# Forgetting-attention layer of a streaming trunk on one core: every matmul on 128 rows and columns, one softmax for four heads' new tokens, z before the next q, and output transpositions beside the last chunks

## The reference

```python
def fox_attend(q, f_q, q_pos, k, v, f_k, k_pos):
    s = jnp.einsum('bqhd,bkhd->bhqk', q, k).astype(jnp.float32) * (B_HEAD_DIM ** -0.5)
    s = s + jnp.transpose(f_q, (0, 2, 1))[..., :, None] - jnp.transpose(f_k, (0, 2, 1))[..., None, :]
    s = jnp.where(k_pos[None, :] <= q_pos[:, None], s, -jnp.inf)
    p = jax.nn.softmax(s, axis=-1)
    return jnp.einsum('bhqk,bkhd->bqhd', p.astype(v.dtype), v)

def fox_layer(x, ...):
    q, z = jnp.split(rmsnorm(x, norm_g) @ w_in, 2, axis=-1)      # w_in 2048 x 4096
    q = rmsnorm(q.reshape(bsz, seq, B_HEADS, B_HEAD_DIM), q_norm_g)  # 16 heads of 128
    ...
    y = (o * jax.nn.silu(z)) @ w_out                              # w_out 2048 x 2048
    return x + y.astype(x.dtype)
```

## Time and profile before

| | |
|---|---|
| median of 3 runs | 1923.48 us (1923.11 to 1923.82) |
| profiled execution: its own time | 1920.44 us |
| its span (first to last instruction) | 1918.6 us |
| PE busy | 1840.1 us (96% of the span) |
| DVE, ACT, POOL busy | 1074.2, 828.8, 290.3 us |
| mean granted TensorE clock (1 is 2.4 GHz) | 0.976 |
| first and last product matmul of the attention layer | 1409.6 and 1907.5 us |

### The profile page before, as it was taken

How to read it: one execution, slowest core, us unless ns; L and a number is a source line. 1 busy time by engine, 2 the same in 40 slices (tenths; PEclk the granted TensorE clock), 3 DMA queues, 4 the chain that set the end, 5 groups by cost and what they waited for, 6 DMA issues and landing times. The chain is left out here.

```text
span 1918.6 us, 29975 instructions
## 1 busy us (share of the span) xinstructions
PE 1840.1 (96%) x12128; PEld 1675.5 (87%) x12128; DVE 1074.2 (56%) x2021; ACT 828.8 (43%) x1406; POOL 290.3 (15%) x569
## 2 busy tenths in 40 slices
PE   4999999999998999999999999999979999999998
PEld 2998889988887999999999899999977798989877
DVE  4565546554546666667757667554355355454544
ACT  4344344534444434434524435545544353443432
POOL 1001111111132321322321210211010000000000
PEclk9999999999999999999999999999989799999998
DMA  3454445644484665655656644465672354535422
GB/s 103 153 169 156 158 142 162 190 144 154 123 249 138 213 211 169 219 190 173 222 175 188 211 132 141 153 212 160 209 248 88 95 157 128 161 107 158 140 75 72
DMA packets 243305, 309.28 MB, mean 161 GB/s; under 512 B 13864, under 2 KB 219456, under 8 KB 242864
## 3 DMA queue, kind: packets, MB, share of 16 engines
q1 hardware_dynamic: 213232, 213.35, 36.4%
q0 software_dynamic: 29232, 91.24, 14.0%
q10 hardware_dynamic: 704, 2.79, 0.5%
HBM read 260.53 MB, written 46.79 MB: 160 GB/s over the span
## 5 line engine op out<-in xcount | busy, mean ns | idle before, releaser
L157 DVE TENSOR_TENSOR w_lo<-raw,w_hi 128x1024 fp32r<-128x1024 f32 x400 | 484.4, 1220 | 421.9 <-ACT w_hi L152 420.4
L152 ACT ACTIVATE w_hi<-raw 128x1024 fp32r<-128x1024 f32 x400 | 412.1, 1053 | 125.4 <-PE acc L177 118.3
L175 PE MATMUL acc<-xg_hi,w_hi 128*128 128x304 f32 x1024 | 315.9, 308 | 4.7 <-DVE w_lo L157 4.7
L177 PE MATMUL acc<-xg_hi,w_lo 128*128 128x304 f32 x1024 | 309.3, 302 | 0.0
L176 PE MATMUL acc<-xg_lo,w_hi 128*128 128x304 f32 x1024 | 309.2, 302 | 0.0
L104 POOL TENSOR_TENSOR cell<-cell 1x1 f32<-1x1 f32 x154 | 65.3, 424 | 1314.8 <-issue 282.5
L175 PEld LDWEIGHTS acc<-xg_hi,w_hi 128*128 128x128 f32 x1024 | 193.3, 189 | 7.9 <-DVE w_lo L157 6.0
L176 PEld LDWEIGHTS acc<-xg_lo,w_hi 128*128 128x128 f32 x1024 | 194.0, 189 | 0.8
L177 PEld LDWEIGHTS acc<-xg_hi,w_lo 128*128 128x128 f32 x1024 | 193.6, 189 | 0.0
L175 PE MATMUL acc<-xb_hi,w_hi 128*128 128x288 f32 x512 | 157.2, 307 | 8.7 <-DVE xb_lo L2340 8.7
L175 PE MATMUL acc<-xk_hi,w_hi 128*128 128x304 f32 x512 | 157.7, 308 | 3.7 <-DVE xk_lo L1879 3.7
(11 more groups left out here) (471 smaller groups left out, 3777.3 us busy)
## 6 DMA issues: line engine op xcount, KB each, us to landing
raw<-in_a_w_in SPq DMA_DIRECT2D x128, 512.0 KB, 4.0
raw<-in_a_w_out SPq DMA_DIRECT2D x64, 512.0 KB, 4.5
raw<-in_w_kvf SPq DMA_DIRECT2D x64, 512.0 KB, 4.5
raw<-in_b_w_in SPq DMA_DIRECT2D x64, 512.0 KB, 3.8
raw<-in_b_w_out SPq DMA_DIRECT2D x32, 512.0 KB, 3.6
raw<-in_a_wq SPq DMA_DIRECT2D x16, 512.0 KB, 4.1
raw<-in_a_wk SPq DMA_DIRECT2D x16, 512.0 KB, 3.6
raw<-in_a_wv SPq DMA_DIRECT2D x16, 512.0 KB, 4.4
```

The lines of the kernel that those rows point to most:

```text
L152: act.activation(w_hi[:, s, :, :], raw[:, s, :, :], ACT.Copy).then_inc(hi_made, 1)
L157: dve.tensor_tensor(w_lo[:, s, :, :], raw[:, s, :, :], w_hi[:, s, :, :].bitcast(F32), ALU.subtract).then_inc(lo_made, 1)
L175: pe.matmul(acc[b][:, 0:width], wh, x_hi[:, k0 + k, :], start=st, stop=False)
L177: mm = pe.matmul(acc[b][:, 0:width], wl, x_hi[:, k0 + k, :], start=False, stop=last and k == 3)
```

## The change

- Order of chunks: q_0, then for each group z_g, OUT_(g-1) (none for g = 0), q_(g+1) (none for g = 3), and OUT_3 at the end. Group g's events now lie in slots 0 to 14 from the first z chunk on.
- The new tokens' scores of four heads are one event Y: q of head x is put into zero-padded columns (`q_new2`), so that its 128-column weights give rows 32x to 32x+31, and the four heads accumulate in one bank. One softmax (EY, NY) and one set of five transpositions (TY) serve all four heads. X takes the place of S and forms the prompt scores alone.
- T has five full 128 x 128 transpositions; O has two matmuls of 256 columns, four of 32 and one of 160.
- The third block of q holds tokens 160 to 287 (128 rows) in place of 32 rows; b uses three banks in place of five; f uses 12 `scalar_tensor_tensor` in place of six `tensor_tensor`.
- All four K events come in slots 1 and 2.
- The last group's high and low parts (H) go to buffers of their own and lie in slots 9 to 15; the others' in slots 0 and 1 of the next group.
- The 48 transpositions of the result are four events y0 to y3 beside the last eight chunks, in the `aux` banks, with no block between.

```diff
-        BESIDE = {8: ["q"], 9: ["r"], 10: ["n"], 11: ["f"], 12: ["K0"], 13: ["b"], ...
+        BESIDE = {0: "q", 1: "r n K0 K1", 2: "f K2 K3", 3: "b", 4: "X0 Y", 5: "E0 EY", 6: "N0 NY X1",
+                  7: "T0 E1 TY", 8: "z O0 N1 X2", 9: "T1 E2", 10: "O1 N2 X3", 11: "T2 E3", 12: "O2 N3", 13: "T3",
+                  14: "O3"}
+        PARTS_NEXT = {0: "H0 H1", 1: "H2 H3"}
+        PARTS_LAST = {9: "H0", 11: "H1", 13: "H2", 15: "H3"}
+        Y_OUT = {2: "y0", 4: "y1", 6: "y2", 7: "y3"}
...
                 def q_finals(g):
...
-                    for t, (_, n) in enumerate(QT):
-                        y = qst[0:n, 3, GRP * t:GRP * (t + 1)].unsqueeze(2).to_broadcast([n, GRP, P])
-                        own.done(dve.tensor_tensor(head_parts(q_t[0:n, t, :], n), head_parts(q_t[0:n, t, :], n), y, ALU.mult))
-                    own.wait()
-                    for t, (_, n) in enumerate(QT):
-                        dve.tensor_tensor(q_t[0:n, t, :], q_t[0:n, t, :], gq[0:n, :], ALU.mult).then_inc(q_final, 1)
+                    for t in range(3):
+                        for m in range(GRP):
+                            d = slice(m * P, (m + 1) * P)
+                            k = GRP * t + m
+                            ins = dve.scalar_tensor_tensor(q_t[:, t, d], q_t[:, t, d], qst[:, 3, k:k + 1], gq[:, d],
+                                                           ALU.mult, ALU.mult)
+                        ins.then_inc(q_final, 1)
...
+                def scores(g, x):
...
+                    bank = free_bank(use(g, f"X{x}"))
+                    for c, w, t0 in ((CA, WA, 0), (CB, WB, P)):
+                        pe.matmul(bank[:, c:c + w], sel[:, x, :], F2[:, FP:FP + w], start=True, stop=False)
+                        pe.matmul(bank[:, c + w - P:c + w], ident_bf[:, :], tri[:, :], start=False, stop=False)
+                        mm = pe.matmul(bank[:, c:c + w], qT[:, x, t0:t0 + P], kT_in[:, x, 0:w], start=False, stop=True)
+                    mm.then_inc(use_ready, 1)
+
+                def scores_new(g):
...
+                    pe.matmul(bank[:, 0:PAST], of_all, F2[:, FC:FC + PAST], start=True, stop=False)
+                    for x in range(GRP):
+                        mm = pe.matmul(bank[:, 0:PAST], q_new2[:, x * P:(x + 1) * P], KcT[:, x, :], start=False,
+                                       stop=x == GRP - 1)
+                    mm.then_inc(use_ready, 1)
+                    bank = free_bank(u + 1)
+                    pe.matmul(bank[:, 0:WZ], of_all, F2[:, FN:FN + WZ], start=True, stop=False)
+                    pe.matmul(bank[:, 0:WZ], ident_bf[:, :], tri_new[:, :], start=False, stop=False)
+                    for x in range(GRP):
+                        mm = pe.matmul(bank[:, 0:WZ], q_new2[:, x * P:(x + 1) * P], kT_in[:, x, 256:T], start=False,
+                                       stop=x == GRP - 1)
+                    mm.then_inc(use_ready, 1)
...
+                def turn_probs(g, x):
+                    u = use(g, f"T{x}")
+                    pe.wait_ge(probs_ready, GRP * g + x + 1)
+                    bank = free_bank(u)
+                    for c, k in enumerate((0, 2, 1, 3)):
+                        mm = pe.transpose(bank[:, c * P:(c + 1) * P], Pf[:, k * P:(k + 1) * P], ident[:, :])
+                    mm.then_inc(use_ready, 1)
+                    pe.transpose(free_bank(u + 1)[:, 0:P], Pf[:, 4 * P:5 * P], ident[:, :]).then_inc(use_ready, 1)
+
+                def turn_probs_new(g):
...
+                    pe.transpose(free_bank(u + 1)[:, 0:P], Ps[:, PAST:PAST + P], ident[:, :]).then_inc(use_ready, 1)
...
+                    pe.matmul(bank[:, 0:256], v_all[:, 0, d], PT[:, 0:256], start=True, stop=False)
+                    pe.matmul(bank[:, 0:256], v_all[:, 1, d], PT[:, 256:512], start=False, stop=True)
+                    for s in range(4):
+                        pe.matmul(bank[:, 256:TQ], Vc[:, s, d], PTs[:, s, x * DEC:(x + 1) * DEC], start=False,
+                              stop=False, skip_group_check=True)
+                    pe.matmul(bank[:, P:TQ], v_all[:, 2, d], PT2[:, x, :], start=False, stop=True,
+                              skip_group_check=True).then_inc(use_ready, 1)
...
+                dve.memset(v_all[:, 2, :], 0.0)
+                dve.memset(F2[:, :].bitcast(F32), 0.0).then_inc(f_set, 1)
                 low_x(0)
                 low_x(4)
-                dve.memset(F2[:, :].bitcast(F32), 0.0).then_inc(f_set, 1)
```

More of the change, by code:

```diff
@@ new lines, in trunk, with add @@
+        BESIDE = {0: "q", 1: "r n K0 K1", 2: "f K2 K3", 3: "b", 4: "X0 Y", 5: "E0 EY", 6: "N0 NY X1",
[4 more added lines that the diff above has]
+        Y_OUT = {2: "y0", 4: "y1", 6: "y2", 7: "y3"}
+        order, at = [], A_FOX
+        def add(kind, g):
+            global_at = at
+            for j in range(8):
+                tile = global_at + (2 * j if kind == "OUT" else 2 * (j // 4))
+                order.append((Count(C_FOX + len(order)), kind, g, j, Count(tile), []))
+            return global_at + (16 if kind == "OUT" else 4)
@@ new lines, in trunk @@
+        at = add("Q", 0)
+        for g in range(GROUPS):
+            first = len(order)
+            at = add("Z", g)
+            if g:
+                at = add("OUT", g - 1)
+            if g < LAST_G:
+                at = add("Q", g + 1)
+            for k, slot in enumerate(order[first:]):
+                if g:
+                    slot[5].extend((g - 1, e) for e in PARTS_NEXT.get(k, "").split())
+                slot[5].extend((g, e) for e in BESIDE.get(k, "").split())
+                if g == LAST_G:
+                    slot[5].extend((g, e) for e in PARTS_LAST.get(k, "").split())
@@ new lines, in trunk @@
+        first = len(order)
+        at = add("OUT", LAST_G)
+        for k, slot in enumerate(order[first:]):
+            slot[5].extend((LAST_G, e) for e in Y_OUT.get(k, "").split())
+        assert len(order) == 24 * GROUPS
+        USE, uses = {}, 0
+        TILE = {(kind, g): tile.a for _, kind, g, j, tile, _ in order if j == 0}
+        for *_, events in order:
+            for g, e in events:
+                USE[g, e] = uses
+                uses += {"q": 3, "b": 3, "K": 1, "X": 1, "Y": 2, "T": 2, "O": 1, "y": 3}.get(e[0], 0)
@@ L2068, in _, with use, freed, written @@
+        def use(g, e, k=0):
+            return USE[g, e] + k
+        def freed(eng, u):
+            eng.wait_ge(use_free[u % 4], u // 4 + 1)
+        def written(eng, u):
+            eng.wait_ge(use_ready, u + 1)
+        with nc.Block() as block:
             @block.sync
             def _(sp):
[L2070 to L2075, removed]
@@ L2133, in q_by_token @@
                 def q_by_token(g):
-                    for t, (_, n) in enumerate(QT):
+                    for t in range(3):
                         u = use(g, "q", t)
[L2137 to L2141, removed]
+                        written(act, u)
+                        act.activation(q_t[:, t, :], aux[u % 4][:, :], ACT.Copy,
+                                       scale=rcol[:, 1, t:t + 1]).then_inc(use_free[u % 4], 1)
+                        freed(act, u)
+                        act.activation(q_sq[:, t, :], q_t[:, t, :], ACT.Square).then_inc(q_squared, 1)
@@ L2364, in _ @@
                 own.done(dve.tensor_scalar(minus[0:BH, :], ident[0:BH, 0:BH], -1.0, None, ALU.mult))
                 own.done(dve.tensor_scalar(minus[32:32 + BH, :], ident[32:32 + BH, 32:32 + BH], -1.0, None, ALU.mult))
+                for r in (32, 64, 96):
+                    own.done(dve.tensor_copy(tri_new[r:r + 32, :], tri_new[0:32, :]))
                 own.wait()
-                turns(Count(0), True, chunk, event)
-                for k in range(1, GROUPS):
-                    turns(Count(k), False, chunk, event)
@@ L2370, in _ @@
-                last = Count(GROUPS - 1)
-                for e in ("O2", "N3", "O3"):
-                    event(last, e)
-                for m in range(GRP):
-                    low_oz(last, m)
-                for n, j, tile in last_steps:
-                    if n.a + 2 < C_END:
-                        low_part(dve, n + 2)
-                    add_out(n, j, tile)
+                for n, kind, g, j, tile, events in order:
+                    if n.a + 2 < C_FOX + len(order):
+                        low_part(dve, n + 2)
+                    if (kind, g) == ("Q", 0):
+                        if j < 2:
+                            low_x(8 + 4 * j)
+                        if j == 2:
+                            dve.wait_ge(F_high, 1)
+                            dve.tensor_tensor(F2[32:32 + BH, :], F_row[:, :], F2[0:BH, :].bitcast(F32),
+                                              ALU.subtract).then_inc(F_low, 1)
+                    if kind == "Z" and j in (3, 7):
+                        take_z(g, n, j, tile)
+                    if kind == "OUT":
+                        add_out(n, j, tile)
+                    for e in events:
+                        event(*e)
```

(24 more changed lines are left out.)

576 lines of the change are left out of this document (251 added, 325 removed).

## The result

The change makes the kernel 3.2% faster: 1861.07 us (median of 4 runs, 1860.88 to 1862.68) against 1923.65, ratio 0.9678 with a 95% interval of 0.9667 to 0.969. I forecast 1898.3 with a range of 1881 to 1914. The sign was right, the size was not: the gain is 62.6 us, not 25.2, and the time lies outside the range. In the later runs the kernel before took 1921.5 to 1922.4 us, so a difference from 1861.07 is uncertain by about 2 us; where that matters, distances from one start to the next in the traces decide.

A forecast was written before the change was run, and what follows sets the result against it. PE was taken as the bound (busy 115.5 of 117.0 us in group 1). Work -22.8, waits and start +13.3, clock -15, end -4.8, moved transpositions +4.1 sum to -25.2 us: median 1898.3 us, range 1881 to 1914.

The forecast's parts named there:

- Work of PE, per group: Matmuls and transpositions at full clock: scores save 1.59 us, T 2.07, O 2.04; 5.7 per group, -22.8 us in all.
- Padding the forget term: In the scores' matmuls: going from 48 to 128 rows changes no column count, so X stays at 1.72 us.
- My bounds: On PE's matmul prices: 256 columns cost 0.36 to 0.98 us (-6 to +13); 512 columns 0.98 to 1.25 (+4).
- The clock: PE's time lost to low granted clock falls from 26 us to 11 (8 after b's wait, 3 elsewhere): -15 us.
- The wait at b: PE waits at b for f's q_t blocks, 4.8 us per group (4.1 in group 0); rounded up to 20 us.
- TY: New PE wait in slot 7 for the bank that E1 frees: 1.3 us per group, 5.2 us (3 to 8).
- H3: Before the last OUT chunk row, its low part stands behind chunk 15's add: a wait of 1.4 us.
- The tail: From the last product to the span's end: 6.3 us instead of 11.1, -4.8 us.
- the 36 transpositions: Result transpositions moved from the end into PE's full stream: +4.1 us.
- B: Rival: no wait at b, as f gets through sooner; without wait and low clock 1870 us; chance 0.12.
- C: Rival: clock stays low after b through chunk 4, X0 and Y; 1918 us, or 1909 by group 0's loss; chance 0.18.
- D: Rival: low clock lasts from b to T0 in each group, 36 us more, 1934 us; chance 0.05.

The follow-up runs named there:

- experiment 1: Changed kernel with X's two forget-term matmuls per head back on 48 rows: 1870.96 us (+9.9); on 112 rows instead: 1862.96 us.

## Why the prediction was wrong, step by step

**The step that failed** is "Work of PE, per group": its prices were taken from start to start in the trace before and carried over by shape. A distance from one start to the next holds what the change of rows to the next matmul costs, and the change took these changes of rows away. Padding the forget term, I wrote, "changes no column count", and so costs and saves nothing; it saves 0.6 us per head (9.9/16 in experiment 1). In figures, per group: scores saved 14.0 - 4 x 1.06 - 4.82 = 4.9 us (I had 1.6), T 2.4 (2.1), O 4 x 1.20 = 4.8 (2.0). Together 12.1 instead of 5.7, over four groups 48 instead of 22.8 (Y's 512-column matmuls alone took 3.03/4 = 0.76 us each and not the 0.98 of the sum): **25 of the 37 us** by which I was off. My bounds did not help, as I bounded each shape by other shapes in the same stream. The hint was there: the forget term of 144 columns at 1571.53 took 0.26 us to the next start (1571.79, shown above), a product of 288 columns 3.30/24 = 0.14. The failed term is thus a mechanism that the sum lacked, and not a wait or an overlap between engines.

**The clock.** I had 26 us before and 11 after. Of the 11, 3 were for narrow stretches, which no longer exist, and 8 for low levels after b's wait. These came in every group, but they lay mostly under the wait itself. Group 1 (PE waits from 1539.0 to 1542.7, then b):

```profile
1542.60:1543.60 1.00, 0.88 (x4) 0.67 (x4) 1.00 (x5) 0.54 (x1) 0.00 (x0) 0.61 0.88 310
1543.60:1544.60 1.00, 1.00 (x5) 0.71 (x4) 1.00 (x5) 0.00 (x0) 0.00 (x0) 0.50 0.06 19
1544.60:1545.60 1.00, 1.00 (x7) 0.78 (x5) 1.00 (x2) 0.00 (x0) 0.74 (x1) 0.50 0.00 0
1545.60:1546.60 1.00, 1.00 (x7) 1.00 (x6) 1.00 (x4) 0.00 (x0) 0.86 (x2) 0.68 0.07 16
1546.60:1547.60 1.00, 1.00 (x10) 1.00 (x9) 1.00 (x3) 0.00 (x0) 0.00 (x0) 1.00 0.40 88
```

The level is low for about 3.4 us, and for most of it PE only turns q and waits for the next block of it. The chunk behind took 3.6 to 4.2 us instead of 3.3, in sum 2.7 us over the four groups; with b's last four transpositions (0.77 us instead of 0.41, in each group) some 4, not 11: **some 7 us**.

**The wait at b** was right to the step: first `q_t` block at +16.4 us by my chain, +16.5 in the trace (1526.24 to 1542.72), f's end at +18.5 in both. DVE's timeline shows the two places where it queued, w_lo behind ACT's K copies and f behind w_lo:

```profile
1539.36 1.23 DVE L157 TENSOR_TENSOR w_lo<-raw,w_hi 128x1024 fp32r<-128x1024 f32 x1 [3.26 <-ACT w_hi L152]
...
1541.53 3.24 DVE L2302 SCALAR_TENSOR_TENSOR q_t<-q_t,qst,gq 128x128 f32<-128x128 f32 x12
```

The four first waits sum to 14.0 us. Then b itself takes 2.87 us from its first transposition to the chunk, where q's 12 take 1.23, because f's blocks come 1.05 us apart: 20.6 us in all, 1.4 of them the slow last transpositions counted above, so 19.2 against the 20 forecast. TY took 4.6 against 5.2, H3 1.3 against 1.4. **Together 1 to 2 us** of the miss.

**The tail** took 5.9 us from the last product to the end (1854.9 to 1860.8) against 6.3 forecast, 11.1 before. With the 36 transpositions beside the chunks (3.7 us against 4.1) that is another 1 us. Some 2 us of the 37 are not placed.

**Rivals.** B (no wait at b), C (the clock stays low through Y) and D did not happen. No rival said that an unchanged matmul gets cheaper when its neighbour gets wider, although the change pads nearly all of them.

What stays open: what lets the clock fall in one kernel and not in another with the same instructions and waits just ahead of it; how much of the clock's gain from before to after comes from the padding, and how much from the chunks beside the events; whether the rows count by 32 or by 64; and what columns do.

## What to carry to other kernels

In a stream of matmuls on this engine keep the rows the same from one to the next, padding with zeros if need be, or put narrow ones side by side: each narrow matmul between wide ones costs 0.3 to 0.4 us more here, more than many of the matmuls themselves. Price a matmul from a stream in which its neighbours look as they will after the change, and read the start of the next weight load beside it. When a chain over several engines limits an order of slots, as q to b here, add up its steps from the trace: it came out within 0.1 us, and one slot of distance more was worth 14 us.

## What the runs showed of the hardware that I had not expected

- A change of rows between two matmuls costs time. The same 144-column matmul took 0.39 us to the next start with 48 rows behind it and 0.21 with 128, and the next weight load started 0.39 or 0.18 us after its start. From O's last matmul to X's first it was 0.24 us with 128 rows in both, 0.44 and 0.47 with 48 in one of them, 0.27 with 48 in both. 112 rows behave as 128.
- TensorE's granted clock stayed at 1.00 through 20 us in which PE was busy for 73% of the time, and fell to 0.50 after the same two pairs of waits in a kernel that differed by two kinds of 48-row matmuls. The first fall came 7.9 us after the last of these. The cause is not shown.
